# Full-attention scores as two 128-row products and one 32-row product a chunk of keys

## The reference

```python
def one_block(qblk):
    s = jnp.einsum('bqhd,bkhd->bhqk', qblk, k_all, preferred_element_type=jnp.float32) * MLA_SCALE
    p = jax.nn.softmax(s, axis=-1).astype(v_all.dtype)
    return jnp.einsum('bhqk,bkhd->bqhd', p, v_all)
```

## Time and profile before

| | us |
|---|---|
| median of 3 runs | 1368.01 |
| lowest and highest | 1366.71, 1368.48 |
| the profiled execution, its own time | 1368.91 |
| its span, first to last instruction | 1367.1 |
| PE busy | 1325.3 (97%) |
| DVE busy | 1022.8 (75%) |
| ACT busy | 737.6 (54%) |

### The profile page before, as it was taken

The page is one execution under the profiler, slowest core; times in us unless marked ns, Lnnn a source line. Parts: engine busy times, 40 slices in busy tenths (PEclk is TensorE's granted clock), DMA queues, the critical chain, the costliest instruction groups (busy, mean ns, idle before and its releaser), DMA issues.

```text
span 1367.1 us, 18988 instructions
## 1 busy us (share of the span) xinstructions
PE 1325.3 (97%) x7118; PEld 1121.9 (82%) x7118; DVE 1022.8 (75%) x1396; ACT 737.6 (54%) x1405; POOL 507.2 (37%) x331
## 2 busy tenths in 40 slices
PE   5899998999999999999999999999999999999998
PEld 1688887899888988898888888888888888888886
DVE  1878777787777877876687796767687776868678
ACT  2756565788877876984223543444353535344440
POOL 2766564021199995411000031404123231404333
PEclk8999999999999999999999999999999999999999
DMA  9555657533056564401334535527261735437043
GB/s 374 195 159 172 177 165 236 197 91 88 20 215 197 153 205 154 107 19 32 93 108 139 170 104 211 193 90 270 81 237 62 251 119 211 159 124 246 31 185 123
DMA packets 149130, 210.55 MB, mean 154 GB/s; under 512 B 10136, under 2 KB 101144, under 8 KB 146224
## 3 DMA queue, kind: packets, MB, share of 16 engines
q1 hardware_dynamic: 144432, 200.91, 45.2%
q10 hardware_dynamic: 4352, 8.39, 1.7%
q0 software_dynamic: 256, 0.05, 0.0%
HBM read 162.90 MB, written 44.32 MB: 152 GB/s over the span
## 4 chain that ended last, share of the span: by engine, by line
PE 74%; DVE 15%; ACT 7%; DMA 2%; issue 2%; SPq 0%; POOL 0%; DVEq 0%; ACTq 0%
PE f_ps L2728 19%; PE f_ps L2691 17%; PE a_ps L1428 7%; PE o_ps L1776 6%; PE a_ps L1444 6%; PE a_ps L1474 5%; PE f_ps L2259 5%; ACT s_pr L1525 3%; PE t_ps L956 2%; DVE s_nmx L1610 2%; PE t_ps L945 2%; DMA t_wm<-in_w_mod 1%; PE f_ps L2744 1%; PE t_ps L971 1%; DVE f_fin L2536 1%
## 5 line engine op out<-in xcount | busy, mean ns | idle before, releaser
L2239 POOL TENSOR_TENSOR f_wr<-f_wr,f_wr 128x1024 f32<-128x1024 f32 x24 | 61.8, 2575 | 285.7 <-DMA f_wr<-in_w_mlp 157.0
L2728 PE MATMUL f_ps<-f_bh,f_ah 128*128 128x512 f32 x392 | 152.6, 389 | 0.6 <-DVE mix L2562 0.6
L2728 PE MATMUL f_ps<-f_bh,f_al 128*128 128x512 f32 x392 | 152.5, 389 | 0.0
L2728 PE MATMUL f_ps<-f_bl,f_ah 128*128 128x512 f32 x392 | 152.5, 389 | 0.0
L1624 DVE TENSOR_TENSOR l_pT<-a_ps,l_pT 128x512 fp32r<-128x512 f32 (+1 forms) x192 | 108.9, 594 | 53.2 <-ACT l_pT L1535 53.1
L2560 DVE TENSOR_TENSOR mix<-mix,f_ps 128x512 f32<-128x512 f32 x180 | 116.5, 681 | 37.6 <-PE f_ps L2728 37.3
L1428 PE MATMUL a_ps<-l_k,l_q 96*128 96x512 f32 (+1 forms) x576 | 136.4, 366 | 0.5 <-DVE l_mo L1636 0.5
L956 PE MATMUL t_ps<-w_in,t_h 128*128 128x416 f32 (+2 forms) x600 | 125.8, 356 | 0.3 <-DVE w_in L719 0.3
L1535 ACT ACTIVATE l_pT<-a_ps 128x512 fp32r<-128x512 f32 (+1 forms) x192 | 95.0, 525 | 39.5 <-PE a_ps L1444 39.2
L1542 ACT ACTIVATE l_pr<-a_ps,l_nb 128x256 f32<-128x256 f32 (+1 forms) x128 | 100.5, 790 | 12.5 <-DVE l_nb L1615 10.0
L1428 PEld LDWEIGHTS a_ps<-l_k,l_q 96*128 96x128 f32 x576 | 95.3, 189 | 12.4 <-DVE l_mo L1636 0.7
(11 more groups left out here) (251 smaller groups left out, 2953.6 us busy)
## 6 DMA issues: line engine op xcount, KB each, us to landing
f_hq<-scratch_hs SPq DMA_DIRECT2D x64, 512.0 KB, 5.4
l_wg<-in_w_mod SPq DMA_DIRECT2D x8, 2048.0 KB, 8.5
f_w<-in_w_mlp SPq DMA_DIRECT2D x16, 1024.0 KB, 7.5
f_ring<-scratch_hs SPq DMA_DIRECT2D x32, 512.0 KB, 5.4
f_wr<-in_w_mlp SPq DMA_DIRECT2D x24, 512.0 KB, 3.9
t_wm<-in_w_mod SPq DMA_DIRECT2D x8, 1024.0 KB, 12.8
scratch_k<-t_kT SPq DMA_DIRECT2D x20, 384.0 KB, 3.7
l_k<-scratch_k SPq DMA_DIRECT2D x8, 960.0 KB, 10.4
```

The source lines that it names most:

```text
L2728: last = nc.tensor.matmul(ps[:, b, :], op_a[s][x][:, f, t * P:(t + 1) * P], op_b[s][w][:, f, :], start=(i in (M1, M2, M5) and f == 0 and k ...
```

## The change

The products q0·k0, q0·k1 and q1·k0 have 3 × 96 = 288 rows in all. They are packed anew as 128 + 128 + 32 rows. The buffers of q and k have 128 partitions now: in layer 0 the 96 rows of q0 and the first 32 of q0 again, against the 96 of k0 and the first 32 of k1; in layer 1 the last 64 rows of q0 and the first 64 of q1, against the last 64 of k1 and the first 64 of k0. The 32 rows that are left (q1 against k0) lie in new tiles `qC` and `kC`, three times: for the chunk of keys 0 to 511 on partitions 0 to 31, for 512 to 1023 on 32 to 63, for 1024 to 1279 on 64 to 95. Those three products, one for each chunk, are issued behind each other when all six of 128 rows are. Each step has nine score products, as before. The pair of transposes stands behind the first chunk's two products of 128 rows; before, it stood behind its three of 96.

All steps cut the keys in the same way now, so `full_exp` only gets other addresses. `load(h)` has 15 transfers where it had 3; for heads 0 and 1 they are spread over four banded units each. The new tiles use room "X".

```diff
-        qT.append(room(f"l_q{b}", [QK, 2, SEQ], F32R))
-        kT.append(room(f"l_k{b}", [QK, 2, KALL], F32R))
+        qT.append(room(f"l_q{b}", [P, 2, SEQ], F32R))
+        kT.append(room(f"l_k{b}", [P, 2, KALL], F32R))
+        qC.append(far(f"l_qc{b}", [QK, SEQ], F32R))
+        kC.append(far(f"l_kc{b}", [QK, BANK], F32R))
...
+    CUT = ((0, 512), (512, 1024), (1024, KALL))
+    LOADS = 15
...
-            sp.dma_start(qT[b][:, :, :].bitcast(F32), scr["q"][h, :, :, CTX:KALL]).then_inc(loaded[b], 16)
-            sp.dma_start(kT[b][:, :, :].bitcast(F32), scr["k"][h]).then_inc(loaded[b], 16)
-            sp.dma_start(vm[b][:, :, :].bitcast(F32), scr["v"][h].rearrange("t p c -> p t c")).then_inc(loaded[b], 16)
+            q, k = scr["q"][h, :, :, CTX:KALL], scr["k"][h]
+            if not parts or 0 in parts:
+                sp.dma_start(qT[b][0:QK, 0, :].bitcast(F32), q[:, 0, :]).then_inc(loaded[b], 16)
+                sp.dma_start(qT[b][QK:P, 0, :].bitcast(F32), q[0:P - QK, 0, :]).then_inc(loaded[b], 16)
+                sp.dma_start(qT[b][0:64, 1, :].bitcast(F32), q[P - QK:QK, 0, :]).then_inc(loaded[b], 16)
+                sp.dma_start(qT[b][64:P, 1, :].bitcast(F32), q[0:64, 1, :]).then_inc(loaded[b], 16)
+            if not parts or 1 in parts:
...
+            if not parts or 2 in parts:
+                for i, (lo, hi) in enumerate(CUT):
+                    sp.dma_start(qC[b][32 * i:32 * i + 32, :].bitcast(F32), q[64:QK, 1, :]).then_inc(loaded[b], 16)
+                    sp.dma_start(kC[b][32 * i:32 * i + 32, 0:hi - lo].bitcast(F32), k[64:QK, 0, lo:hi]).then_inc(loaded[b], 16)
+            if not parts or 3 in parts:
+                sp.dma_start(vm[b][:, :, :].bitcast(F32), scr["v"][h].rearrange("t p c -> p t c")).then_inc(loaded[b], 16)
...
-            if u == 4:
-                load(0)
-            if u == 8:
-                load(1)
+            if 4 <= u < 12:
+                load((u - 4) // 4, u % 4)
...
-                pe.wait_ge(loaded[b], 48 * (h // 2 + 1))
+                pe.wait_ge(loaded[b], 16 * LOADS * (h // 2 + 1))
...
-            cut = ((0, 0, 512), (512, 512, 1024), (1024, 1024, 1280)) if s % 2 == 0 else \
-                ((1536, 256, 768), (2048, 768, 1280), (1280, 0, 256))
-            for c, (a0, lo, hi) in enumerate(cut):
+            starts = (0, 512, 1024) if s % 2 == 0 else (1536, 2048, 1280)
+            rows = slice(qt * P, (qt + 1) * P)
+            for c, (a0, (lo, hi)) in enumerate(zip(starts, CUT)):
                 if c == 1 and s != SUM_AT:
                     third_fill(s - 2)
                 if c == 2:
                     pe.wait_ge(shared_read, s)
-                for i, (a, w) in enumerate(((0, 0), (0, 1), (1, 0))):
-                    last = MM(fps[:, a0:a0 + hi - lo], qT[b][:, a, qt * P:(qt + 1) * P], kT[b][:, w, lo:hi],
-                              start=(i == 0), stop=(i == 2))
+                for i in range(2):
+                    MM(fps[:, a0:a0 + hi - lo], qT[b][:, i, rows], kT[b][:, i, lo:hi], start=(i == 0), stop=False)
+            for c, (a0, (lo, hi)) in enumerate(zip(starts, CUT)):
+                third = slice(32 * c, 32 * c + 32)
+                last = MM(fps[:, a0:a0 + hi - lo], qC[b][third, rows], kC[b][third, 0:hi - lo], start=False, stop=True)
             last.then_inc(scored, 1)
```

More of the change, by code:

```diff
@@ L1096, in attention_phase @@
     room = Z.room("L")
-    qT, kT, vm = [], [], []
+    far = Z.room("X")
+    qT, kT, qC, kC, vm = [], [], [], [], []
     for b in range(2):
-        qT.append(room(f"l_q{b}", [QK, 2, SEQ], F32R))
-        kT.append(room(f"l_k{b}", [QK, 2, KALL], F32R))
+        qT.append(room(f"l_q{b}", [P, 2, SEQ], F32R))
+        kT.append(room(f"l_k{b}", [P, 2, KALL], F32R))
+        qC.append(far(f"l_qc{b}", [QK, SEQ], F32R))
+        kC.append(far(f"l_kc{b}", [QK, BANK], F32R))
         vm.append(room(f"l_v{b}", [P, NT, P], F32R))
@@ L1277, in sync, with load @@
     def sync():
-        def load(h):
+        def load(h, *parts):
             b = h % 2
-            sp.dma_start(qT[b][:, :, :].bitcast(F32), scr["q"][h, :, :, CTX:KALL]).then_inc(loaded[b], 16)
-            sp.dma_start(kT[b][:, :, :].bitcast(F32), scr["k"][h]).then_inc(loaded[b], 16)
-            sp.dma_start(vm[b][:, :, :].bitcast(F32), scr["v"][h].rearrange("t p c -> p t c")).then_inc(loaded[b], 16)
+            q, k = scr["q"][h, :, :, CTX:KALL], scr["k"][h]
[5 more added lines that the diff above has]
+            if not parts or 1 in parts:
+                sp.dma_start(kT[b][0:QK, 0, :].bitcast(F32), k[:, 0, :]).then_inc(loaded[b], 16)
+                sp.dma_start(kT[b][QK:P, 0, :].bitcast(F32), k[0:P - QK, 1, :]).then_inc(loaded[b], 16)
+                sp.dma_start(kT[b][0:64, 1, :].bitcast(F32), k[P - QK:QK, 1, :]).then_inc(loaded[b], 16)
+                sp.dma_start(kT[b][64:P, 1, :].bitcast(F32), k[0:64, 0, :]).then_inc(loaded[b], 16)
+            if not parts or 2 in parts:
[4 more added lines that the diff above has]
+                sp.dma_start(vm[b][:, :, :].bitcast(F32), scr["v"][h].rearrange("t p c -> p t c")).then_inc(loaded[b], 16)
         def load_gate(k):
@@ L1538, in full_exp @@
             act.wait_ge(shift_ready, s + 1)
[L1539 to L1542, removed]
+            m, odd = s - W, s % 2
+            halves = ((1024, KALL), (0, 1024))
+            starts = (1280, 1536) if odd else (1024, 0)
+            for i, ((lo, hi), a0, done) in enumerate(zip(halves, starts, (shared_read, exped))):
+                nc.scalar.activation(l_pr[:, odd, lo:hi], fps[:, a0:a0 + hi - lo], ACT.Exp, bias=nb[:, odd:odd + 1],
                                      accum_out=l_sums[:, i, m % NB, m // NB:m // NB + 1]).then_inc(done, 1)
```

## The result

The changed kernel takes 1372.46 us (median of 5; 1369.92 to 1374.29) against 1368.15 (median of 5) for the one before: ratio 1.0031, 95% interval 1.0017 to 1.0046. Forecast were 1372.8 us and slower by more than 0.2%. Both hold, though the lower end of the interval lies just under 0.2%. Of the two terms of the forecast only one was there.

A forecast was written before the change was run, and what follows sets the result against it. It took VectorE's and ScalarE's loop to set the pace in odd pairs, level with TensorE in even ones. Moved transposes (+2.2) and head 6's load (+2.6) gave +4.8 us: 1373.7 on the profiled execution, 1372.8 median; range 1366.5 to 1390.

The forecast's parts named there:

- the two terms of the forecast: Moved transposes in the full attention, +2.2 us, and head 6's later load, +2.6 us.
- The bound: Full attention: VectorE and ScalarE set the pace by 0.15 us in odd pairs; level with TensorE in even pairs.
- the other two engines' loop: VectorE's and ScalarE's maximum, exponential, third parts and output addition: two-step period 8.23 us in odd pairs, 8.08 in even.
- Score products: TensorE's scores in each step: row groups overlap, but switches take the saving; 1.75 us before and after.
- the two switches: TensorE's array going into the small shape, 0.19 us, and out of it, 0.16: 0.35 us a step.
- The pair of transposes: 0.23 us of TensorE work moves behind the wait for VectorE: +0.07 us in each of 32 pairs, +2.2 us.
- the sum of the loop through the transposes: Maximum, transposes, high parts, exponential, output, next maximum in odd pairs: 8.07 us before, 8.30 with 0.23 more, against 8.23.
- The loads: 1120 KB more a head, landing 4.8 us later: hidden except at head 6, where TensorE waits, +2.6 us.
- ScalarE's wait for the gate's stores: At head 6 the stores stand behind its load; ScalarE waits at much the same time, not counted twice.

The follow-up runs named there:

- e1: Kernel before, with the third score product (low part of q by high part of k) left out everywhere in the full attention: 1364.95 us, ratio 0.9975.
- e8: Kernel before, with VectorE's maximum over the first 640 columns only and a square for ScalarE's exponential: 1366.75 us.
- e3: Changed kernel with all three 32-row products on the first third's operands, so in one row group: 1385.85 us, ratio 1.0128.
- e9: e5 with a maximum over 640 columns only and a square for the exponential: 1363.97 us.
- e7: e5, with ScalarE carrying an odd head's half over and VectorE adding on partitions 64 to 127 alone: 1369.02 us.
- e4: Kernel before, with the pair of transposes behind two products of the first chunk instead of three: 1369.77 us, ratio 1.001.
- e2: Kernel before, with the change's 15 transfers and 1120 KB more a head, products untouched: 1373.2 us, ratio 1.003.
- e5: Changed kernel with two of eight output-weight transfers ahead of head 6's load, the other six behind the gate's stores: 1367.76 us, ratio 0.9994.
- e10: Kernel before, with even heads' outputs written to partitions 64 to 127 and odd heads' to 0 to 63: 1368.09 us.
- e6: Kernel before, with ScalarE carrying an odd head's half over and VectorE adding on partitions 64 to 127 alone: 1368.49 us.

## Why the prediction was right, and where it was not

**The bound.** Right, by e1, and e8 gives the margin: TensorE's own pair is 8.08 us, against 8.22 and 8.05 for the other two engines' loop. In even pairs TensorE is thus the longer one by 0.03 us, which the prediction called level.

**Score products.** Right: row groups overlap (e3), the step is the same length (8.06 for 8.08 a pair in e9 and e8). So the two switches together cost the 0.35 us that the column groups' rows gave, since that is what the products saved. The rule cited from the Trainium skill, page "TensorE: Matmul & The Clock Gate", "Part 3: Packing small matmuls — row/col tiling", that small products in different row groups run concurrently, holds here: 0.43 us for 0.78. That of "TensorEngine Tiling (Array Packing)", "Tiling Modes", that a change of mode drains the array, agrees with the 0.24 us idle behind the three products.

**The pair of transposes.** Wrong in size: +2.2 us forecast, 0 measured. The step that failed is the sum of the loop through the transposes, 8.07 before and 8.30 after. Read from the changed trace the links are: maximum to load 2.14, load to the next transposes' load 1.50, to the high parts 0.69, to the exponential 1.02, then 1.97 + 0.46 + 0.45 as before. That they add up to 8.23 proves nothing, since starts read once round a period always do. What counts is the shortest that each link can be. The prediction had taken 1.09 for the high parts, their whole record; the exponential can follow them after 0.97 (e8, e3), because neighbouring records overlap. In the changed kernel it follows after 1.02, with the end of the maximum. So the loop needs 8.18, the other one takes 8.22, and the 0.23 us found room. The rest of the step was right: from the pair's load to the high parts it takes 2.19 us for 1.95 before, the 0.23 and no less. And where one link more is 0.11 longer, in e7, the same loop sets the pace at 8.32. That e4 measured +0.07 does not save the term: there the same size came through another wait, of the maximum for the scores.

**The loads.** The mechanism and the delay were right (4.9 us for 4.8), and the place, head 6 alone. The term was too small, +2.6 for 4.3 us. It counted only TensorE's wait, and that was 2.05 us: the load started 1.45 us earlier than before and TensorE came to the place 0.8 us earlier. ScalarE's wait for the gate's stores, which the prediction named and left uncounted, was longer (3.10 us) and held up work that TensorE needed next, and the granted clock then fell for some 4 us. e2 and e5 show that this place is all of the loss.

So the time of 1372.8 was met by luck: a term that was not there (2.2) stood for what another lacked (1.7).

## What to carry to other kernels

A TensorE that is always busy, and a chain of waits that never leaves it, do not prove that it is the bound. Follow the other engines' own loop over one period and see if every link starts as the one before ends; a period that changes with something that only another engine does gives it away. To price a loop that has slack, take for each link the shortest distance that any step shows, not the length of its record: 0.12 us of one record turned a free move into a forecast loss here. Before a change that buys products with copies, find the load with the least time to spare: 1.1 MB more a head was hidden at all heads but one and was the whole loss there. Packing products into small row groups pays when more is saved than two switches of the array, 0.35 us here; with three small products a step it only came out even.

## What was not expected of the hardware

- A wait of TensorE of 2 us was followed by 4 us at a granted clock of 0.60 and 0.55. In e2 a wait of 3.11 us was followed by 0.50 over 6 us. In e8 two waits of 1.04 and 0.72 us, 0.96 us of work between them, were followed by 0.73, 0.50 and 0.91 in stretches of 2 us.
- VectorE's next instruction starts 0.45 us after the start of an addition that writes partitions 64 to 127, and 0.34 us after the same addition on partitions 0 to 63 (e10); it is 0.46 where all its operands lie on the upper partitions (e6).
- A pattern fits all of VectorE's late starts: an instruction starts before its forerunner's record ends (0.34 and 0.40 for 0.42, 1.41 for 1.49) unless the partitions that it reads or writes start elsewhere than the last ones did; then it starts behind that end (0.45 and 0.46 for 0.42, and in e6 and e7, where the addition also reads from partition 64, 1.52 for 1.49). It is read off these runs, and none was made to test it.
- Weight loads of 32 rows and 128 columns in three row groups take 0.19 us together (changed kernel); in one row group the three take 0.53 us (e3).
